# Forgetting attention on one core: the keys' low parts as two 64-row products side by side, pieces of a query tile in groups of two

## The chip, the cores and the metric

One core of a Trainium2 chip runs the whole kernel. The metric is device time in microseconds. The kernel before took 1963.35 us (median of 3 runs, 1961.30 to 1967.77); the profiled execution took 1961.69 us, with a span of 1960.3 us in the trace.

## What is computed

One layer of a hybrid decoder trunk on x of 2048 tokens by 1024 channels. The input projection feeds three mixers (trailing-window pooling, attention with a forget gate, a state-space layer), whose outputs are gated, lifted, merged and projected back, with a residual and a layer norm. The change touches the attention alone: 8 heads of 64 channels, causal, 128 queries at a time.

```python
scores = einsum('bqhd,bkhd->bhqk', qi, k) * scale        # scale = 1/sqrt(64)
bias = F[q] - F[k]                                       # F = cumsum(log sigmoid(f))
logits = where(key_pos <= q_pos, scores + bias, -inf)
p = softmax(logits)
out = einsum('bhqk,bkhd->bqhd', p, v)
```

## The kernel before

**Stages.** Three stages run one after the other: the projection with pooling and state space (until about 616 us), the attention (616 to 1552 us), and the merge with the output projection (to the end). The attention stage also carries 24 tiles of the gate projection in each of two phases: its matmuls fill the gaps that the attention leaves on TensorE, by a table of counts for each slot between the attention's steps (`fill_plan`, and `fill` in `head`). These fills write `g_ps`, 24 matmuls to a bank, each 128 rows by 512 columns.

**Split numbers.** Each fp32 operand is split in a high part that the fp32r format holds and a low part that is the rest. A product is high times high, plus high times low, plus low times high.

**Score products.** With 64 channels to a head, the 128 rows of the array hold a query tile twice. `q_st` has the high part of the scaled queries in rows 0 to 63 and their low part in rows 64 to 127. `k_hh` has the keys' high part in both halves, `k_ll` their low part in both halves. So one matmul `q_st` x `k_hh` (L1329) gives (high + low) x high, and a second one `q_st` x `k_ll` (L1330) adds (high + low) x low. Both have 128 rows. `q_tmp` is a third tile: its rows 64 to 127 hold the high part of the scaled queries, and serve only to work out the low part. `vT` lies in rows 0 to 63 of the same memory.

**Query tiles and pieces.** Query tile t (0 to 15) has (t + 1) * 128 keys, cut into pieces of 512 keys (`pieces`); the last piece can be 128, 256, 384 or 512 wide. That is one piece for t = 0 to 3, two for 4 to 7, three for 8 to 11, four for 12 to 15: 40 pieces to a head. A piece has a PSUM bank `s_ps` of three in turn. In `queries` (L1322 and on) TensorE waits until the bank is free, makes the two products, adds the causal mask to the tile's last 128 keys by a bf16 matmul with the identity (L1334), and signals `s_full`.

**The order around it.** In `head`, the loop over t has on TensorE, in this order: `queries` of tile t + 1, its first three pieces (L1412); the fills of slot (t, 0), eight or nine matmuls from t = 2 on; `queries` of tile t + 1, its fourth piece (L1415); for even t from 2 the products with the values of a pair of tiles (`values`, L1359, writing `o_ps`, closed by two transposes of `row_inv`, L1364); then `turn`, which transposes the probabilities of tile t by groups of four 128 by 128 fp32 transposes (L1345, writing `t_ps`, two banks in turn), with three fills between groups. The head begins with tile 0's queries, 16 transposes of `vT` (L1404), which has 64 rows only, and, in the second phase, the first fills.

**The other engines.** VectorE subtracts the key's forget sum from each piece and takes its maximum (`logits`, L1240, written to `s_sb`); it does all pieces of tile t + 1 before anything that it does for tile t's transposes. Behind them come the negated maximum (L1244), in some slots the split of a weight tile (L1230), then the low parts of the transposed probabilities (L1302), one for each piece, each after ScalarE's high part (L1208). ScalarE also takes the exponentials (L1199). The transposes of piece j in `turn` wait for the low part of the piece two before (the semaphore `t_lo`).

Of the kernel before, what the change touches and what calls it, by code (L numbers as in the profile page):

```python
# [25 lines left out]
P = 128  # L26
# [8 lines left out]
HD = 64  # L35
# [931 lines left out]
Q_TILES = S // P  # L967
# [8 lines left out]
def stage_attend(nc, io, scr, kept, ident, ident_b, mask, x_hi, x_lo, x_raw, gw_hi, gw_lo, gw_raw):  # L976
# [4 lines left out]
    with ExitStack() as ctx:  # L981
        def sb(name, shape, dt=F32):
            return ctx.enter_context(nc.sbuf_tensor(name, shape, dt))
# [6 lines left out]
        k_hh = sb("k_hh", [P, S], F32R)  # L990
        k_ll, q_st, q_tmp, vT, f_row = kept.k_ll, kept.q_st, kept.q_tmp, kept.vT, kept.f_row
# [10 lines left out]
        s_ps = [ctx.enter_context(nc.psum_tensor(f"s_ps{i}", [P, BANK], F32)) for i in range(3)]  # L1002
# [20 lines left out]
        def pieces(t):  # L1023

            n0 = sum(-(-(a + 1) // 4) for a in range(t))
            keys = (t + 1) * P
            return [(n0 + j, j * BANK, min(BANK, keys - j * BANK)) for j in range(-(-keys // BANK))]
# [5 lines left out]
        def pieces_to(t):  # L1033

            return pieces(t)[-1][0] + 1
# [284 lines left out]
        @block.tensor  # L1320
        def _(pe):
            def queries(at, t, part=slice(None)):  # L1322

                for n, k0, keys in pieces(t)[part]:
                    if n >= 3:
                        pe.wait_ge(s_free, at(S_PIECES, n - 2))
                    ps = s_ps[n % 3][:, 0:keys]
                    last_piece = k0 + keys == (t + 1) * P
                    pe.matmul(ps, q_st[:, t * P:(t + 1) * P], k_hh[:, k0:k0 + keys], start=True, stop=False)  # L1329
                    last = pe.matmul(ps, q_st[:, t * P:(t + 1) * P], k_ll[:, k0:k0 + keys], start=False,  # L1330
                                     stop=not last_piece)
                    if last_piece:

                        last = pe.matmul(ps[:, keys - P:keys], ident_b[:], mask[:], start=False, stop=True)  # L1334
                    last.then_inc(s_full, 1)

            def turn(at, t, fill):

                pe.wait_ge(p_ready, at(Q_TILES, t + 1))
                for j, (n, k0, keys) in enumerate(pieces(t)):  # L1340
                    if j:
                        fill((t, j))
                    pe.wait_ge(t_lo, at(PT_USES, n + 1))
                    for a in range(keys // P):
                        last = pe.transpose(t_ps[n % 2][:, a * P:(a + 1) * P],  # L1345
                                            s_sb[t % 2][:, k0 + a * P:k0 + (a + 1) * P], ident[:])
                    last.then_inc(t_full, 1)

            def values(at, p):

                pe.wait_ge(t_lo, at(PT_USES, pieces_to(2 * p + 1) + 2))
                if p:
                    pe.wait_ge(y_ready, at(8, p))
                last_key = 2 * p + 1
                for k in range(last_key + 1):

                    q = slice(P, 2 * P) if k == last_key else slice(0, 2 * P)
                    for j, pt in enumerate((pt_hi, pt_lo)):
                        pe.matmul(o_ps[:, 0, q], v_st[:, k, :], pt[:, k, q], start=(k == 0 and j == 0),  # L1359
                                  stop=(k == last_key and j == 1))  # L1360
                pe.wait_ge(inv_ready, at(8, p + 1))
                pe.sem_inc(passed[2])
                for a in range(2):
                    last = pe.transpose(o_ps[0:HD, 1, a * P:(a + 1) * P],  # L1364
                                        row_inv[:, 2 * p + a:2 * p + a + 1].broadcast_to([P, HD]), ident[:])
                last.then_inc(o_full, 1)

            def head(at, phase):

                    filled = [0]  # L1370

                    def fill(slot):
                        for _ in range(fill_counts[slot]):
                            piece, r = divmod(filled[0], 3 * KT)
                            j, c = divmod(piece, NCH)

                            k, (w, x) = ((r, (gw_hi, x_lo)) if r < KT else
                                         ((r - KT) // 2, ((gw_hi, x_hi), (gw_lo, x_hi))[(r - KT) % 2]))
                            filled[0] += 1
                            if r == 0:  # L1380
                                if c == 0:
                                    pe.wait_ge(gw_split, at(G_TILES, j + 1))
                                pe.wait_ge(g_ready, at(G_TILES * NCH, piece + 1))
                            if phase == 1 and j == 0 and r < KT:
                                pe.wait_ge(x2_split, c * KT + k + 1)
                            mm = pe.matmul(g_ps[c][:], w[j % 2][:, k, :], x[:, k, c * BANK:(c + 1) * BANK],  # L1386
                                           start=(r == 0), stop=(r == 3 * KT - 1))
                            if r == KT - 1:
                                mm.then_inc(x_lo_used, 1)
                            if r == 3 * KT - 1:  # L1390
                                mm.then_inc(g_done, 1)

                    if phase == 0:
                        fill("start")
                    pe.wait_ge(k_lo, at(1, 1))
                    pe.wait_ge(q_hi, at(1, 1))
                    pe.wait_ge(q_lo, at(1, 1))
                    queries(at, 0)
                    pe.wait_ge(v_loaded, at(16, 16))
                    pe.sem_inc(passed[2])  # L1400
                    for b in range(2):
                        for t in range(8):
                            k = 8 * b + t
                            last = pe.transpose(t_ps[b][:, t * HD:(t + 1) * HD], vT[:, k * P:(k + 1) * P],  # L1404
                                                ident[0:HD, 0:HD])
                        last.then_inc(t_full, 1)
                    if phase == 1:
                        fill("start")
                    for t in range(Q_TILES):

                        if t + 1 < Q_TILES:
                            queries(at, t + 1, slice(0, 3))  # L1412
                        fill((t, 0))
                        if t + 1 < Q_TILES:
                            queries(at, t + 1, slice(3, 4))  # L1415
                        if t % 2 == 0 and t >= 2:
                            values(at, t // 2 - 1)
                        turn(at, t, fill)
                    fill("end")
                    values(at, 7)  # L1420
                    fill("tail")

            pe.sem_inc(g_ready, NCH)  # L1423
            for phase in range(2):
                with pe.Fori(0, PHASE_HEADS - phase) as i:
                    head(lambda k, c: i * k + (c + phase * PHASE_HEADS * k), phase)
            head(lambda k, c: (HEADS - 1) * k + c, 1)


# [455 lines left out]
```

## Time and profile before

| | |
|---|---|
| median of 3 runs | 1963.35 us |
| profiled execution, its time | 1961.69 us |
| its span in the trace | 1960.3 us |
| TensorE, busy share of the span | 98% |
| VectorE | 57% |
| ScalarE | 36% |
| GpSimd | 22% |
| granted TensorE clock, mean | 0.995 |

The trace names each matmul (PE) and each weight load (PEld) with its start. A matmul's end is modelled and laps over the next one's start, so what a matmul costs in a dense stretch is the distance from its start to the next start, not its printed duration. The printed shape `128*128 128x512` is the stationary tile (rows*columns), then the moving tile; `64*128` is a stationary tile of 64 rows.

### The profile page before, as it was taken

Reading aid. Unit: us, or ns where it says so; the run is one execution under the profiler, and the core shown is the slowest. Engines: PE = TensorE matmul, PEld = TensorE weight load, DVE = VectorE, ACT = ScalarE, POOL = GpSimd, SP = SyncE. Lnnn points to the kernel's source line nnn. Section 1 sums busy time; section 2 is a strip of 40 time slices with the busy share of each in tenths; the row PEclk is TensorE's granted clock in tenths of the full one; section 3 lists DMA queues with packets and bytes.
Section 4 is the critical chain, followed back from the end, with each engine's and each line's share of the span. In section 5 each row is a group of like instructions: output and inputs, shape, how many; then the busy total and the mean of one; then the engine's idle time right before and its main releaser. Section 6 shows DMA issues by size and latency. Waiting matters only on the chain. (4 is left out here: it accounts for less than half of the span.)

```text
span 1960.3 us, 30528 instructions
## 1 busy us (share of the span) xinstructions
PE 1913.3 (98%) x10560; PEld 1623.1 (83%) x10560; DVE 1124.5 (57%) x2133; ACT 706.6 (36%) x1081; POOL 435.0 (22%) x548
## 2 busy tenths in 40 slices
PE   7999999999999999999999999999999989999998
PEld 6878887888887888888888788888888878999997
DVE  4564235654245655646465665565645568777776
ACT  3121013021034555555555655455555541111110
POOL 2927930498000000000000000000000002222322
PEclk9999999999999999999999999999999989999999
DMA  7124225322432151231423515133142276555542
GB/s 190 67 86 118 86 86 196 63 107 107 139 109 93 49 139 54 80 110 47 138 68 87 175 48 139 62 87 109 49 128 66 91 251 209 170 173 171 174 118 86
DMA packets 103479, 221.68 MB, mean 113 GB/s; under 512 B 10936, under 2 KB 56680, under 8 KB 99816
## 3 DMA queue, kind: packets, MB, share of 16 engines
q1 hardware_dynamic: 89648, 161.41, 26.2%
q0 software_dynamic: 12608, 55.19, 10.1%
q10 hardware_dynamic: 1152, 4.19, 0.5%
q8 instruction: 37, 0.61, 0.1%
q14 instruction: 34, 0.28, 0.0%
HBM read 155.09 MB, written 65.08 MB: 112 GB/s over the span
## 5 line engine op out<-in xcount | busy, mean ns | idle before, releaser
L1386 PE MATMUL g_ps<-x_hi,w_lo 128*128 128x512 f32 x768 | 309.4, 403 | 0.0
L1386 PE MATMUL g_ps<-x_hi,w_hi 128*128 128x512 f32 x768 | 308.4, 402 | 0.0
L1302 DVE TENSOR_TENSOR pt_lo<-t_ps,pt_hi 128x512 fp32r<-128x512 f32 (+2 forms) x320 | 190.4, 606 | 138.2 <-ACT pt_hi L1208 137.8
L643 PE MATMUL tile_ps<-x_hi,w_hi 128*128 128x512 f32 x752 | 234.1, 393 | 11.2 <-DVE x_lo L362 11.2
L643 PE MATMUL tile_ps<-x_hi,w_lo 128*128 128x512 f32 x752 | 232.1, 390 | 0.0
L643 PE MATMUL tile_ps<-x_lo,w_hi 128*128 128x512 f32 x752 | 232.0, 390 | 0.0
L1386 PE MATMUL g_ps<-x_lo,w_hi 128*128 128x512 f32 x768 | 225.9, 410 | 3.9 <-PEq L1423 2.6
L1208 ACT ACTIVATE pt_hi<-t_ps 128x512 fp32r<-128x512 f32 (+2 forms) x320 | 170.4, 533 | 142.4 <-PE t_ps L1345 137.9
L1240 DVE CUSTOM_DVE_ANT_0 s_sb<-s_ps,f_row 128x512 f32<-128x512 f32 (+2 forms) x320 | 181.6, 604 | 35.1 <-PE s_ps L1334 34.4
L1116 POOL DMA_DIRECT2D mixT<-y_out x63 | 33.8, 536 | 748.1 <-DVE y_out L1254 748.1
L1345 PE MATMUL t_ps<-ident,s_sb 128*128 128x128 f32 x1088 | 172.1, 273 | 9.6 <-DVE pt_lo L1302 5.2
L643 PEld LDWEIGHTS tile_ps<-x_hi,w_hi 128*128 128x128 f32 x752 | 141.1, 188 | 41.5 <-issue 12.6
L1345 PEld LDWEIGHTS t_ps<-ident,s_sb 128*128 128x128 f32 x1088 | 133.2, 140 | 47.1 <-DVE pt_lo L1302 10.8
L280 ACT ACTIVATE w_hi<-w_lo_raw 128x1024 fp32r<-128x1024 f32 x49 | 52.0, 1061 | 319.9 <-DMA w_lo_raw<-in_w_tiles 319.9
L1386 PEld LDWEIGHTS g_ps<-x_hi,w_lo 128*128 128x128 f32 x768 | 145.4, 189 | 24.9
L643 PEld LDWEIGHTS tile_ps<-x_lo,w_hi 128*128 128x128 f32 x752 | 141.4, 188 | 29.6
L643 PEld LDWEIGHTS tile_ps<-x_hi,w_lo 128*128 128x128 f32 x752 | 141.5, 188 | 29.5
L1386 PEld LDWEIGHTS g_ps<-x_hi,w_hi 128*128 128x128 f32 x768 | 145.4, 189 | 24.6
L1386 PEld LDWEIGHTS g_ps<-x_lo,w_hi 128*128 128x128 f32 x768 | 136.3, 190 | 28.5 <-PEq L1423 3.1
L1199 ACT ACTIVATE s_sb<-s_sb,neg_max 128x128 f32<-128x128 f32 (+15 forms) x128 | 153.3, 1197 | 6.7 <-DVE neg_max L1244 6.6
L1733 PE MATMUL u_ps<-y_hi,wu_hi 128*128 128x256 f32 x512 | 146.1, 285 | 9.0 <-DVE gate L1662 6.4
L1733 PE MATMUL u_ps<-y_lo,wu_hi 128*128 128x256 f32 x512 | 146.0, 285 | 0.0
(276 smaller groups left out, 3537.4 us busy)
## 6 DMA issues: line engine op xcount, KB each, us to landing
w_lo_raw<-in_w_tiles SPq DMA_DIRECT2D x96, 512.0 KB, 3.6
gateT<-g_out SPq DMA_DIRECT2D x96, 256.0 KB, 3.0
gate<-gateT SPq DMA_DIRECT2D x64, 384.0 KB, 4.5
x_lo_raw<-in_xT SPq DMA_DIRECT2D x24, 512.0 KB, 8.4
qkvT<-zout SPq DMA_DIRECT2D x24, 512.0 KB, 3.2
silT<-zout SPq DMA_DIRECT2D x16, 512.0 KB, 2.7
k_ll<-qkvT POOLq DMA_DIRECT2D x16, 512.0 KB, 6.7
q_st<-qkvT POOLq DMA_DIRECT2D x16, 512.0 KB, 8.7
```

The source lines that it names most:

```text
L280: act.activation(w_hi[par][:], w_raw[par][:], ACT.Copy).then_inc(w_split_hi, 1)
L643: last = pe.matmul(tile_ps[par][:, c * BANK:(c + 1) * BANK], w[par][:, k, :], x[:, k, c * BANK:(c + 1) * BANK], start=(k == 0 and j == 0), ...
L1116: pool.dma_start(scr["mixT"][bass.ds(row, HD), p * 2 * P:(p + 1) * 2 * P], y_out[p % 2][:]).then_inc(y_stored, 16)
L1199: act.activation(row, row, ACT.Exp, bias=neg_max[t % 2][:], accum_out=row_sum[:, t:t + 1]).then_inc(p_ready, 1)
L1208: act.activation(pt_hi[:, k0 // P:(k0 + keys) // P, (t % 2) * P:(t % 2 + 1) * P], t_ps[n % 2][:, 0:keys].rearrange("p (k q) -> p k q", q=P ...
L1240: dve.tensor_tensor_reduce(s_sb[t % 2][:, k0:k0 + keys], s_ps[n % 3][:, 0:keys], f_row[:, k0:k0 + keys], 1.0, -3e38, ALU.subtract, ALU.max ...
L1302: dve.tensor_tensor(pt_lo[part], t_ps[n % 2][:, 0:keys].rearrange("p (k q) -> p k q", q=P), pt_hi[part].bitcast(F32), ALU.subtract).then_i ...
L1345: last = pe.transpose(t_ps[n % 2][:, a * P:(a + 1) * P], s_sb[t % 2][:, k0 + a * P:k0 + (a + 1) * P], ident[:])
L1386: mm = pe.matmul(g_ps[c][:], w[j % 2][:, k, :], x[:, k, c * BANK:(c + 1) * BANK], start=(r == 0), stop=(r == 3 * KT - 1))
L1733: mm = pe.matmul(u_ps[d % 2][:, n, :], w, y[:, k, :], start=(k == k0 and j == 0), stop=(k == k1 - 1 and j == 2))
```

## The change

`queries` takes the pieces of a call as a group. First it makes the products with `k_hh` of all pieces of the group, 128 rows each, as before. Then, where the group has one piece, the product with `k_ll` follows as before. Where it has two, the keys' low part is multiplied with the queries' high part alone: for the first piece in rows 0 to 63 (stationary from `q_st`), for the second in rows 64 to 127 (stationary from `q_tmp`). The product low times low is left out there. The mask follows at the end. The calls in `head` take pieces 0 and 1 ahead of the fills of slot (t, 0), and pieces 2 and 3 behind them, where it was 0 to 2 and 3.

```diff
             def queries(at, t, part=slice(None)):
 
-                for n, k0, keys in pieces(t)[part]:
+                group, q = pieces(t)[part], slice(t * P, (t + 1) * P)
+                for n, k0, keys in group:
                     if n >= 3:
                         pe.wait_ge(s_free, at(S_PIECES, n - 2))
+                    pe.matmul(s_ps[n % 3][:, 0:keys], q_st[:, q], k_hh[:, k0:k0 + keys], start=True, stop=False)
+                for i, (n, k0, keys) in enumerate(group):
                     ps = s_ps[n % 3][:, 0:keys]
                     last_piece = k0 + keys == (t + 1) * P
-                    pe.matmul(ps, q_st[:, t * P:(t + 1) * P], k_hh[:, k0:k0 + keys], start=True, stop=False)
-                    last = pe.matmul(ps, q_st[:, t * P:(t + 1) * P], k_ll[:, k0:k0 + keys], start=False,
-                                     stop=not last_piece)
-                    if last_piece:
-
-                        last = pe.matmul(ps[:, keys - P:keys], ident_b[:], mask[:], start=False, stop=True)
-                    last.then_inc(s_full, 1)
+                    if len(group) == 1:
+                        last = pe.matmul(ps, q_st[:, q], k_ll[:, k0:k0 + keys], start=False, stop=not last_piece)
+                    else:
+                        q_hi, rows = ((q_st, slice(0, HD)), (q_tmp, slice(HD, P)))[i]
+                        last = pe.matmul(ps, q_hi[rows, q], k_ll[rows, k0:k0 + keys], start=False, stop=not last_piece)
+                    if not last_piece:
+                        last.then_inc(s_full, 1)
+                n, k0, keys = group[-1]
+                if k0 + keys == (t + 1) * P:
+
+                    pe.matmul(s_ps[n % 3][:, keys - P:keys], ident_b[:], mask[:], start=False, stop=True).then_inc(s_full, 1)
...
                         if t + 1 < Q_TILES:
-                            queries(at, t + 1, slice(0, 3))
+                            queries(at, t + 1, slice(0, 2))
                         fill((t, 0))
-                        if t + 1 < Q_TILES:
-                            queries(at, t + 1, slice(3, 4))
+                        if t + 1 >= 8 and t + 1 < Q_TILES:
+                            queries(at, t + 1, slice(2, 4))
```

On TensorE, tile 5 of a head, whose two pieces are 512 and 256 keys wide (its one group). `s_ps` is the piece's bank. Before:

```order
L1326 REGISTER_ALU
L1329 MATMUL s_ps<-k_hh,q_st 128x512 [waits s_free]
L1330 MATMUL s_ps<-k_ll,q_st 128x512
L1326 REGISTER_ALU
L1329 MATMUL s_ps<-k_hh,q_st 128x256 [waits s_free]
L1330 MATMUL s_ps<-k_ll,q_st 128x256
L1334 MATMUL s_ps<-mask,ident_b 128x128
```

and in the changed program:

```order
L1327 REGISTER_ALU
L1328 MATMUL s_ps<-k_hh,q_st 128x512 [waits s_free]
L1327 REGISTER_ALU
L1328 MATMUL s_ps<-k_hh,q_st 128x256 [waits s_free]
L1336 MATMUL s_ps<-k_ll,q_st 128x512
L1336 MATMUL s_ps<-k_ll,q_tmp 128x256
L1342 MATMUL s_ps<-mask,ident_b 128x128
```

The two products with the low part now stand side by side, behind both products with the high part. The printed shapes are those of the output; the two L1336 matmuls read 64 rows each.

On TensorE, tile 14 of a head, from the last fill of slot (13, 0) to tile 13's first transposes. Before:

```order
L1386 MATMUL g_ps<-x_hi,w_lo 128x512
L1326 REGISTER_ALU
L1329 MATMUL s_ps<-k_hh,q_st 128x384 [waits s_free]
L1330 MATMUL s_ps<-k_ll,q_st 128x384
L1334 MATMUL s_ps<-mask,ident_b 128x128
L1339 REGISTER_ALU
L1343 REGISTER_ALU [waits p_ready]
L1345 MATMUL t_ps<-ident,s_sb 128x128 [waits t_lo]
```

and in the changed program:

```order
L1393 MATMUL g_ps<-x_hi,w_lo 128x512
L1327 REGISTER_ALU
L1328 MATMUL s_ps<-k_hh,q_st 128x512 [waits s_free]
L1327 REGISTER_ALU
L1328 MATMUL s_ps<-k_hh,q_st 128x384 [waits s_free]
L1336 MATMUL s_ps<-k_ll,q_st 128x512
L1336 MATMUL s_ps<-k_ll,q_tmp 128x384
L1342 MATMUL s_ps<-mask,ident_b 128x128
L1346 REGISTER_ALU
L1350 REGISTER_ALU [waits p_ready]
L1352 MATMUL t_ps<-ident,s_sb 128x128 [waits t_lo]
```

The third piece of the tile has moved from ahead of the fills to behind them, directly before the transposes. VectorE's instructions stand in the same order in both programs.

## Rows read from the trace of the kernel before

**Rows 1.** The page, busy time of TensorE, its share, and instructions.

```profile
PE 1913.3 (98%) x10560; PEld 1623.1 (83%) x10560; DVE 1124.5 (57%) x2133; ACT 706.6 (36%) x1081; POOL 435.0 (22%) x548
```

**Rows 2.** Busy time in one stretch (us, engines, then PEclk, DMA): the attention stage.

```profile
616.00:1552.00 936.00, 925.57 (x5379) 779.43 (x5377) 539.92 (x1357) 507.98 (x825) 55.28 (x104) 1.00 0.31 90
```

**Rows 3.** Waits of TensorE, 620 to 1552 us: who, for whom, us, times, longest.

```profile
PE t_ps L1345 <- DVE pt_lo L1302: 5.2, 8, 1.2
PE t_ps L1345 <- ACT s_sb L1199: 3.9, 7, 0.6
```

**Rows 4.** Timeline of PE (start us, duration): scores of tile 14 after a transpose.

```profile
1177.77 0.33 PE L1345 MATMUL t_ps<-ident,s_sb 128*128 128x128 f32 x1
1177.86 0.50 PE L1329 MATMUL s_ps<-k_hh,q_st 128*128 128x512 f32 x1
1178.19 0.39 PE L1330 MATMUL s_ps<-k_ll,q_st 128*128 128x512 f32 x1
1178.42 0.40 PE L1329 MATMUL s_ps<-k_hh,q_st 128*128 128x512 f32 x1
```

**Rows 5.** Timeline of PE: tile 0's scores, then the first 64-row matmul.

```profile
736.60 0.22 PE L1329 MATMUL s_ps<-k_hh,q_st 128*128 128x128 f32 x1
736.66 0.28 PE L1330 MATMUL s_ps<-k_ll,q_st 128*128 128x128 f32 x1
736.78 0.23 PE L1334 MATMUL s_ps<-mask,ident_b 128*128 128x128 bf16 x1
736.94 0.27 PE L1404 MATMUL t_ps<-ident,vT 64*128 64x64 f32 x1
```

**Rows 6.** Timeline of PE: the last three 64-row matmuls, then tile 1's scores.

```profile
737.80 0.34 PE L1404 MATMUL t_ps<-ident,vT 64*128 64x64 f32 x3
738.07 0.39 PE L1329 MATMUL s_ps<-k_hh,q_st 128*128 128x256 f32 x1
738.30 0.28 PE L1330 MATMUL s_ps<-k_ll,q_st 128*128 128x256 f32 x1
738.42 0.23 PE L1334 MATMUL s_ps<-mask,ident_b 128*128 128x128 bf16 x1
```

**Rows 7.** Timeline of weight loads: the first into 64 rows, the first behind them.

```profile
736.94 0.20 PEld L1404 LDWEIGHTS t_ps<-ident,vT 64*128 64x128 f32 x2
...
738.07 0.19 PEld L1329 LDWEIGHTS s_ps<-k_hh,q_st 128*128 128x128 f32 x1
```

**Rows 8.** Timeline of PE: tile 14's last piece, mask, tile 13's first transposes.

```profile
1181.38 0.34 PE L1330 MATMUL s_ps<-k_ll,q_st 128*128 128x384 f32 x1
1181.56 0.23 PE L1334 MATMUL s_ps<-mask,ident_b 128*128 128x128 bf16 x1
1181.63 0.61 PE L1345 MATMUL t_ps<-ident,s_sb 128*128 128x128 f32 x4
```

**Rows 9.** Timeline of weight loads at the places of rows 4 and 8.

```profile
1177.85 0.19 PEld L1329 LDWEIGHTS s_ps<-k_hh,q_st 128*128 128x128 f32 x1
1177.96 0.19 PEld L1330 LDWEIGHTS s_ps<-k_ll,q_st 128*128 128x128 f32 x1
...
1181.57 0.42 PEld L1345 LDWEIGHTS t_ps<-ident,s_sb 128*128 128x128 f32 x4
```

**Rows 10.** Timeline of VectorE around the transposes of tile 13 (in brackets its idle time).

```profile
1179.43 0.69 DVE L1240 CUSTOM_DVE_ANT_0 s_sb<-s_ps,f_row 128x512 f32<-128x512 f32 x1
...
1180.04 0.69 DVE L1240 CUSTOM_DVE_ANT_0 s_sb<-s_ps,f_row 128x512 f32<-128x512 f32 x1
...
1181.98 0.56 DVE L1240 CUSTOM_DVE_ANT_0 s_sb<-s_ps,f_row 128x384 f32<-128x384 f32 x1 [1.25 <-PE s_ps L1334]
...
1182.68 1.23 DVE L1230 TENSOR_TENSOR w_lo<-w_lo_raw,w_hi 128x1024 fp32r<-128x1024 f32 x1
...
1183.90 1.27 DVE L1302 TENSOR_TENSOR pt_lo<-t_ps,pt_hi 128x512 fp32r<-128x512 f32 x2
```

**Rows 11.** Timeline of PE: the third group of transposes of tile 13.

```profile
1184.62 0.66 PE L1345 MATMUL t_ps<-ident,s_sb 128*128 128x128 f32 x4 [0.56 <-DVE pt_lo L1302]
```

## The prediction

> **What bounds the kernel now.** I read the busy shares first. TensorE is busy for 98% of the span [rows 1] and for 925.6 of the 936 us of the attention stage, at the full granted clock of 1.00, which is the 2.4 GHz level [rows 2]; VectorE has 540 us of work there, ScalarE 508. Then the waits: TensorE loses 5.2 us to VectorE's `pt_lo` and 3.9 us to ScalarE's exponentials in the whole stage [rows 3]. So the attention stage is a queue of TensorE work without holes, and what the change takes from or adds to that queue shows in the time one for one. The third view is the timeline of starts, because printed durations lap over each other. A 512-column matmul costs 0.23 us from start to start (1178.19 to 1178.42) [rows 4], a 384-column one 0.18 [rows 8], a 256-column one 0.12 (738.30 to 738.42) [rows 6], a 128-column one 0.06 (736.60 to 736.66) [rows 5]. The fourth view is the weight loads, because the change makes the array go between 128-row and 64-row work, and the trace before has one place in each head that does this: the `vT` transposes.
>
> **How many pairs.** From `pieces`: tiles 4 to 7 give one pair each, tiles 8 to 11 one (the third piece stands alone), tiles 12 to 15 two. That is 16 to a head, 128 in 8 heads. In 80 of them both pieces are 512 wide; in 16 each the second is 384, 256 or 128 wide. 64 pairs (tiles 4 to 7, and the second pair of 12 to 15) are followed by the mask, 64 by another fp32r matmul. Everything else in the stage keeps its matmuls.
>
> **What a pair saves.** If the two halves run side by side, they take as long as the wider one plus the lag of the second. No row shows two 64-row matmuls in different halves. I bound the lag at 0 below and, above, at one exposed fp32r weight load: 0.11 us, by the two loads that follow one another at 1177.85 and 1177.96 [rows 9] and by the 0.23 us that the first 256-column matmul takes at 738.07 where the next takes 0.12 [rows 6]. I take 0.11, since the second load has to follow the first on the same engine.
> - 512 and 512: 0.46 before, 0.23 + 0.11 = 0.34 after, 0.12 saved.
> - 512 and 384: 0.23 + 0.18 = 0.41 before, 0.11 + 0.18 = 0.29 after, 0.12 saved.
> - 512 and 256: 0.35 before, 0.23 after, 0.12 saved.
> - 512 and 128: the 128-wide product takes 0.12 ahead of the mask (736.66 to 736.78) [rows 5], so 0.35 before, 0.23 after, 0.12 saved.
>
> 128 x 0.12 = **15.4 us saved**. With no lag it would be 80 x 0.23 + 16 x (0.18 + 0.12 + 0.12) = 25.1 us.
>
> **What a pair costs: two switches.** Into 64 rows: the mask matmul starts at 736.78, and the first weight load into 64 rows starts only at 736.94, together with its matmul, 0.16 us later [rows 5, 7]. The same mask matmul ahead of full 128-row transposes: 1181.56, then the transpose at 1181.63, 0.07 us later, its weights loading from 1181.57 [rows 8, 9]. So 0.09 us is waited before the load. On top the load itself is exposed: the first `vT` matmul is 0.27 long, and the later ones 0.22 (0.34 for three that start 0.06 apart) [rows 5, 6]: 0.05. Entry: 0.14 us; with a full fp32r load exposed, 0.09 + 0.11 = 0.20. Out of 64 rows: the last `vT` matmul starts at 738.14 - 0.22 = 737.92; the next load and matmul start at 738.07, 0.15 later instead of 0.06 [rows 6, 7], so 0.09 again; and the matmul behind has its load exposed, 0.11 (above). Exit: 0.20 us; into the mask, whose bf16 load is short, I take 0.15 (0.09, and half of the 0.11, rounded up).
>
> Part of the exposed load on the way out may belong to the change from fp32 transposes to fp32r: behind full-height transposes the first score product also takes 0.33 instead of 0.23 (1177.86 to 1178.19) [rows 4]. So the lower bound of a switch is the wait alone, 0.09 each way, 0.18 to a pair; the upper is 0.20 each way, 0.40. I take 0.14 + 0.20 for 64 pairs and 0.14 + 0.15 for 64: 64 x 0.34 + 64 x 0.29 = **40.3 us added**. I stay near the upper bound because in both rows the load did not start before the wait was over, and a load that has not started early is exposed. The bounds are 128 x 0.18 = 23.0 and 128 x 0.40 = 51.2 us.
>
> What I read in these rows is also a rule. The Trainium skill (TensorEngine Tiling (Array Packing), Key Properties) says that changing the tiling mode, not merely the tile, makes TensorE drain. The trace agrees, with 0.09 us of waiting each way. The skill's other page (TensorE: Matmul & The Clock Gate, Measured speedup vs the span model) has row-packed matmuls starting some 4 ns apart and 64-row work overlapping freely; by that figure alone the sum would be an estimated 25 us saved, less about half a microsecond. No run here shows that lag yet.
>
> **What moves.** The products with `k_hh` of a group come first, so the first piece's `s_full` comes some 0.4 us later. VectorE starts later on it, but it idles there for longer than that (1.25 us before 1181.98) [rows 10]. In tiles 8 to 11 the third piece, and in 12 to 15 the third of four, goes behind the eight or nine fills of slot (t, 0). No TensorE work is added by this, but VectorE, which must finish tile t + 1 before tile t's `pt_lo`, gets its last pieces in a bunch. For even t the products with the values, over 2 us, stand behind and cover it. For t = 7, 9 and 11 ScalarE's high part is not ready much before VectorE is free, and the third transpose group is due about 2.4 us after the first (from 1181.63 to 1184.62 less 0.56) [rows 8, 11]: covered, narrowly. For t = 13 it is not: a weight split of 1.23 us stands in VectorE's way, and TensorE already waits 0.56 us [rows 10, 11], once in each head (8 times) [rows 3]. There a 512-wide piece (0.61 us from start to start, 1179.43 to 1180.04 [rows 10]) is added behind the mask: 8 x 0.61 = **4.9 us added**; 0 if VectorE finds slack, twice that if tile 11 stalls too.
> The waits of GpSimd for the head's last `s_full` and `s_free` move with the pieces by less than 1 us; its loads for the next head have the head's end as cover. No DMA, no ScalarE and no VectorE instruction is added. The 3.9 us of waiting for exponentials stand at tile 15, which has no queries behind it, and stay.
>
> **Sum.** -15.4 + 40.3 + 4.9 = +29.8 us on the profiled 1961.69: **1991.5 us**. The median of the runs shown is 1.7 us higher, well under 0.3% (5.9 us), about what a measurement of this kernel can tell from no change. Its own bounds: -25.1 + 23.0 + 0 = -2, and -15.4 + 51.2 + 9.8 = +46; with the terms leaning together only in part, 1972 to 2003.
>
> **Rivals.**
> 1. *The switches are nearly free (faster).* The gaps at the `vT` transposes would come from what surrounds them: a change of data type with unprefetched loads (the full-height transposes show such a 0.10 on the way out [rows 4]) and the wait for `v_loaded`. Two fp32r matmuls of 64 rows behind fp32r ones of 128 would then have none. For it: entry and exit at `vT` are never free of a change of type. Against it: the mask to the full-height transposes is a change of type too and has no 0.16 gap [rows 8]. Time: -15.4 + 4.9 = -10.5, 1951 us; without lag and stall -25, 1937. It decides where a switch costs under 0.06 us (0.12 saved, shared by two).
> 2. *Wash.* A switch costs about 0.09 and the second half starts with little lag: between -6 and +6 us, about 1963.
> 3. *The halves do not overlap (much slower).* If TensorE runs the two 64-row matmuls one after the other, nothing is saved and both switches are paid: 40.3 + 4.9 = +45, 2007 us, up to 2018. Nothing in the trace before speaks for or against; the second matmul's `s_full` would then come a full 0.23 us behind the first's in the 512-wide pairs. That is the case in which the change does not do what it says.
>
> **How the numbers follow.** Switches that cost more than the pair saves: 0.57 (own range 1972 to 2003). Free switches: 0.25. Wash: 0.12. No overlap: 0.06. Slower by over 0.3% takes the first and the last, less a little for the first's low bound, 0.62; the wash gives "same" 0.13 with that; faster 0.25. The range has to reach into the free switches: from 1945 to 2006, which leaves out the lower tail of that rival and most of the last.
>
> **What would show it.** In the changed profile, at a 512 and 512 pair followed by fills: the weight load of the first 64-row matmul starts some 0.3 us behind the start of the second `k_hh` matmul (not within it); the second 64-row matmul starts 0.11 us behind the first; the fill behind has its load start about 0.3 us after the last 64-row matmul. From the start of the second `k_hh` matmul to the second fill I expect about 1.1 us, where the free case gives 0.8. The count of matmuls stays at 10560 and their printed durations change little, so the loss must show in distances and in TensorE's idle or unattributed time. VectorE's `pt_lo` as a releaser of TensorE should go from 5.2 to about 10 us. I am wrong if the load of the 64-row matmul starts inside the matmul ahead of it, or if the two halves start over 0.2 us apart.

## The result, and the profile after

The changed kernel takes 1985.26 us (median of 4 runs, 1984.74 to 1985.63) against 1963.01 us before (four runs now): ratio 1.0107, 95% interval 1.0094 to 1.0120, so 22 us slower. The profiled execution took 1984.74 us with a span of 1983.4 us, 23.1 us over the span before.

The page of the changed kernel, busy times, which answer to [rows 1]:

```profile
PE 1930.5 (97%) x10560; PEld 1592.4 (80%) x10560; DVE 1131.2 (57%) x2133; ACT 706.7 (36%) x1081; POOL 435.5 (22%) x548
```

The same number of matmuls. TensorE's printed busy time rises by only 17 us, and its share falls by a point. Its waits, 620 to 1572 us (who, for whom, us, times, longest), which answer to [rows 3]:

```profile
PE t_ps L1352 <- DVE pt_lo L1302: 8.2, 8, 1.1
PE t_ps L1352 <- ACT s_sb L1199: 3.9, 7, 0.6
```

The named waits grew by 3.0 us. The rest of the 23 us has no releaser, so it must lie in distances between starts. This is the timeline of PE around the two pairs of tile 15 (start us, duration); it answers to [rows 4, 8] with the 64-row matmuls in it. The first two pieces stand ahead of the fills, the last two ahead of the mask and the products with the values:

```profile
1201.28 0.40 PE L1328 MATMUL s_ps<-k_hh,q_st 128*128 128x512 f32 x1
1201.61 0.49 PE L1336 MATMUL s_ps<-k_ll,q_st 64*128 64x512 f32 x1
1201.61 0.50 PE L1336 MATMUL s_ps<-k_ll,q_tmp 64*128 64x512 f32 x1
1202.04 0.50 PE L1393 MATMUL g_ps<-x_hi,w_lo 128*128 128x512 f32 x1
1202.38 0.40 PE L1393 MATMUL g_ps<-x_lo,w_hi 128*128 128x512 f32 x1
...
1204.24 0.39 PE L1328 MATMUL s_ps<-k_hh,q_st 128*128 128x512 f32 x1
1204.56 0.49 PE L1336 MATMUL s_ps<-k_ll,q_st 64*128 64x512 f32 x1
1204.57 0.49 PE L1336 MATMUL s_ps<-k_ll,q_tmp 64*128 64x512 f32 x1
1204.99 0.23 PE L1342 MATMUL s_ps<-mask,ident_b 128*128 128x128 bf16 x1
```

And the weight loads of the same stretch, where "issue" stands for idle time with no releaser:

```profile
1201.61 0.18 PEld L1336 LDWEIGHTS s_ps<-k_ll,q_st 64*128 64x128 f32 x1 [0.36 <-issue]
1201.61 0.18 PEld L1336 LDWEIGHTS s_ps<-k_ll,q_tmp 64*128 64x128 f32 x1
1202.04 0.19 PEld L1393 LDWEIGHTS g_ps<-x_hi,w_lo 128*128 128x128 f32 x1 [0.25 <-issue]
1202.15 1.59 PEld L1393 LDWEIGHTS g_ps<-x_lo,w_hi 128*128 128x128 f32 x7
```

Read it from left to right. The two halves start within 0.01 us of each other, here as in all 128 pairs: they do run side by side. But the weights of the first 64-row matmul are loaded 0.32 to 0.33 us behind the start of the `k_hh` matmul ahead of it, where a matmul that needs no switch starts 0.23 us behind and has had its weights loaded earlier. On the way out the next load starts 0.43 us behind the pair, and the fill it belongs to lasts 0.34 us instead of 0.23 (1202.04 to 1202.38), since its load was exposed. From the second `k_hh` matmul to the second fill it is 1.10 us; before, the same work was one `k_hh`, two `k_ll` and one fill, 4 x 0.23 = 0.92. So this pair loses 0.18 us. Ahead of the mask the pair needs 0.75 us (1204.24 to 1204.99) instead of 0.69, and loses 0.06.

The best ruler for the whole is the distance between two heads. The 16 `vT` transposes stand at a fixed place in each head. Before:

```profile
1337.36 1.20 PE L1404 MATMUL t_ps<-ident,vT 64*128 64x64 f32 x16
1457.92 1.20 PE L1404 MATMUL t_ps<-ident,vT 64*128 64x64 f32 x16
```

and in the changed kernel:

```profile
1355.46 1.20 PE L1411 MATMUL t_ps<-ident,vT 64*128 64x64 f32 x16
1478.87 1.20 PE L1411 MATMUL t_ps<-ident,vT 64*128 64x64 f32 x16
```

A head takes 120.56 us before and 123.41 us after: 2.85 us more. The seven distances between heads grow by 20.2 us together, the last head with all that follows it by 2.1, and what stands ahead of the first head by 0.8. So nearly all of the loss is made in the heads.

The stall at tile 13, in the changed kernel, timeline of PE:

```profile
1198.23 0.40 PE L1393 MATMUL g_ps<-x_hi,w_lo 128*128 128x512 f32 x1
1199.64 0.66 PE L1352 MATMUL t_ps<-ident,s_sb 128*128 128x128 f32 x4 [1.01 <-DVE pt_lo L1302]
```

From the last fill to the transposes it is 1.41 us. Before, that fill stands at

```profile
1183.67 0.40 PE L1386 MATMUL g_ps<-x_hi,w_lo 128*128 128x512 f32 x1
```

and the transposes at 1184.62 [rows 11], 0.95 us. The stall cost 0.46 us more in this head, and as much in each of the first seven. In the last head it was longer before, 1.63 us from start to start, and is 1.46 now. So the stalls grew by 3.0 us in all, as the named waits did.

### The profile page after: what moved, and what is told of

Its sections match the earlier page's. It is cut to its first block and busy times, and to the rows that moved or that the text cites. A ratio compares the mean times of both kernels' runs of the same rounds, so it can differ in the third digit from the quotient of the medians.

```text
span 1983.4 us, 30528 instructions
## 1 busy us (share of the span) xinstructions
PE 1930.5 (97%) x10560; PEld 1592.4 (80%) x10560; DVE 1131.2 (57%) x2133; ACT 706.7 (36%) x1081; POOL 435.5 (22%) x548
```

## The experiments

Each row gives the median, its ratio to the kernel before on the same chip, and the length of a head in the one profile of each kernel (the distance of the last two rows of `vT` transposes, as above). In one profile that length repeats within 0.3 us, but for the two distances around the change of phase and, in the last kernel, the first one.

| kernel | median us | ratio, 95% interval | head, us |
|---|---|---|---|
| before | 1963 to 1964 | 1 | 120.56 |
| changed | 1985.26 | 1.0107, 1.0094 to 1.0120 | 123.41 |
| order only | 1964.96 | 1.0007, 0.9996 to 1.0017 | 120.80 |
| both products in one half | 2006.17 | 1.0218, 1.0201 to 1.0235 | 126.16 |
| pair issued twice | 2014.63 | 1.0259, 1.0241 to 1.0276 | 127.14 |
| 64 rows alone, no pair | 1980.46 | 1.0083, 1.0067 to 1.0100 | 122.64 |
| pairs at the mask only | 1973.68 | 1.0046, 1.0032 to 1.0059 | 121.88 |
| low part first | 1985.57 | 1.0109, 1.0093 to 1.0124 | 123.30 |
| split moved, on before | 1957.03 | 0.9966, 0.9952 to 0.9979 | 119.83 |
| split moved, on changed | 1978.82 | 1.0072, 1.0059 to 1.0086 | 122.32 |
| split and fills moved, on before | 1956.41 | 0.9967, 0.9957 to 0.9977 | 119.71 |

**Order only.** The rival to "the switches cost" was that the new order does. So the changed kernel's order, without a 64-row matmul:

```diff
-                    if len(group) == 1:
+                    if True:
                         last = pe.matmul(ps, q_st[:, q], k_ll[:, k0:k0 + keys], start=False, stop=not last_piece)
```

> The changed kernel's order (groups of two, both products with k_hh first, pieces 2 and 3 behind the fills), but every product with k_ll on all 128 rows, so no 64-row matmul in the scores. Theory (the two switches of the array cost more than the pair saves): only VectorE's stall at tile 13 is left over from the change, 3 us more than before, so 1966 us, and 19 us under the changed kernel. Rival (the loss is the order: VectorE gets its pieces in a bunch and late, and TensorE waits on it in places that the waits do not name): 1980 to 1985 us.

Measured: 1964.96 us, not told apart from the kernel before; the head is 0.24 us longer, 1.9 us in 8. Its waits, 620 to 1620 us:

```profile
PE t_ps L1352 <- DVE pt_lo L1302: 8.1, 8, 1.6
```

The longer stall at tile 13 is there too, and it is all that the order costs: from the last fill to the transposes it is 1.32 us in that kernel's timeline against 0.95 before, 0.37 more. Of this 0.06 and 0.08 us to a head come back ahead of the first transposes of tiles 7 and 9, where a mask that stood ahead of fills now stands directly ahead of the transposes. The 20 us belong to the 64-row matmuls.

**Both products in one half.** Same switches, no overlap:

```diff
-                        q_hi, rows = ((q_st, slice(0, HD)), (q_tmp, slice(HD, P)))[i]
+                        q_hi, rows = (q_st, slice(0, HD))
```

> The changed kernel, but the second 64-row product of a pair also works in rows 0 to 63, so that the two cannot overlap and the count of switches stays. Theory (the halves do overlap fully, lag 0.01 us): each pair gets longer by its second product, 80 x 0.23 + 16 x (0.18 + 0.12 + 0.06) = 24 us, so 2009 us. Rival (they share some port, or the pair is bound by weight loads, and overlap only in part): 1986 to 2000 us.

Measured: 2006.17 us, 21 us over the changed kernel; the head is 2.75 us longer, 22 us in all. That is what the overlap is worth here, close to the 24 expected. 1.6 of the missing 2 us are VectorE's stall, which shrank to 6.6 us. So the pair does what it is meant to do.

**Pair issued twice.** This counts the low-part product of the paired pieces twice, to price a pair without a switch of its own:

```diff
+                if len(group) == 2:
+                    for i, (n, k0, keys) in enumerate(group):
+                        q_hi, rows = ((q_st, slice(0, HD)), (q_tmp, slice(HD, P)))[i]
+                        pe.matmul(s_ps[n % 3][:, 0:keys], q_hi[rows, q], k_ll[rows, k0:k0 + keys], start=False,
+                                  stop=False)
                 for i, (n, k0, keys) in enumerate(group):
```

> The changed kernel with each pair of 64-row products issued twice in a row (the low-part product is counted twice, so the scores are off by one more low-part product). Theory (the cost sits in the two switches, not in the 64-row matmuls): the second pair of halves costs only its streaming, 128 x 0.23 = 29 us, so 2015 us. Rival (each 64-row matmul pays a wait of its own, 0.43 from pair to next load): 128 x 0.43 = 55 us, 2040 us.

Measured: 2014.63 us, on the number; the head is 3.73 us longer, 0.233 us to a pair. The timeline of PE at one of them:

```profile
1218.58 0.49 PE L1332 MATMUL s_ps<-k_ll,q_st 64*128 64x512 f32 x1
1218.59 0.50 PE L1332 MATMUL s_ps<-k_ll,q_tmp 64*128 64x512 f32 x1
1218.92 0.39 PE L1341 MATMUL s_ps<-k_ll,q_st 64*128 64x512 f32 x1
1218.92 0.39 PE L1341 MATMUL s_ps<-k_ll,q_tmp 64*128 64x512 f32 x1
1219.24 0.50 PE L1398 MATMUL g_ps<-x_hi,w_lo 128*128 128x512 f32 x1
```

The first pair takes 0.34 us, the 0.23 of a 512-column matmul and an exposed load. The second takes 0.32 us up to the fill, the same 0.23 and then 0.09 of waiting for the way out. Between the two pairs nothing is lost; the price is paid where 128-row and 64-row work meet.

**64 rows alone.** The disputed price by itself, in the kernel before, where nothing is paired (low times low is left out in these 64 products):

```diff
-                    last = pe.matmul(ps, q_st[:, t * P:(t + 1) * P], k_ll[:, k0:k0 + keys], start=False,
+                    alone = slice(0, HD) if last_piece and (t < 4 or 8 <= t < 12) else slice(None)
+                    last = pe.matmul(ps, q_st[alone, t * P:(t + 1) * P], k_ll[alone, k0:k0 + keys], start=False,
```

> The kernel before, with its own order, where the low-part product of the one piece of tiles 0 to 3 and of the third piece of tiles 8 to 11 is made on 64 rows alone (64 products in all; low times low is left out in them). Nothing is paired and nothing is saved, so this prices two switches by themselves. Theory: for a 512-wide piece 0.32 + 0.43 = 0.75 us from its k_hh product to the mask instead of 0.46, for a 128-wide one 0.42 instead of 0.18; some 0.28 x 64 = 18 us, 1981 us. Rival (switches are nearly free, the loss of the change lies elsewhere): 1963 us.

Measured: 1980.46 us; the head is 2.08 us longer for 8 such products, 0.26 us each. A 512-wide one, timeline of PE:

```profile
1247.11 0.47 PE L1329 MATMUL s_ps<-k_hh,q_st 128*128 128x512 f32 x1
1247.51 0.50 PE L1331 MATMUL s_ps<-k_ll,q_st 64*128 64x512 f32 x1
1247.94 0.23 PE L1335 MATMUL s_ps<-mask,ident_b 128*128 128x128 bf16 x1
```

The same 0.43 us from the 64-row matmul to the mask as in a pair. One 64-row matmul takes as long as a pair, and a switch in and out costs some 0.26 us even ahead of the cheap mask. The rival of free switches is out.

**Pairs at the mask only.** Do all pairs lose alike?

```diff
-                    if len(group) == 1:
+                    if len(group) == 1 or group[-1][1] + group[-1][2] < (t + 1) * P:
```

> The changed kernel with 64-row pairs only where the mask follows (tiles 4 to 7, and pieces 2 and 3 of tiles 12 to 15); the other 64 pairs, all 512 and 512, make their low-part products on 128 rows. Theory (the way out costs less into the bf16 mask than into an fp32r matmul: 0.06, 0.11, 0.17, 0.17 us a pair for a second piece of 512, 384, 256, 128, against 0.17 for the others): 16 x 0.51 = 8.2 us over the order-only kernel, 1973 us. Rival (every pair costs the same, 20 / 128 us): 1975 us; if the pairs with a narrow second piece carry all of the loss: 1983 us.

Measured: the head is 1.08 us longer than in the order-only kernel, 8.6 us in all, 0.135 us a pair; 0.08 us of the 1.08 is the stall at tile 13, which is 1.41 us here as in the changed kernel. The other 64 pairs make up the difference to the changed kernel, 1.53 us a head, 0.19 us a pair. The first agrees with the 8.2 us worked out from the rows, the second with the 0.18 read off above. In time (1973.68 against 1965) the theory and its rival are only 2 us apart, and it is the head's length that tells them apart.

**Low part first.** If a weight load behind the fp32 transposes is exposed anyway, a pair set there should pay for its entry only in part:

```diff
+                two = len(group) == 2 and group[-1][1] + group[-1][2] < (t + 1) * P
+                if two:
+                    for i, (n, k0, keys) in enumerate(group):
...
+                        pe.matmul(s_ps[n % 3][:, 0:keys], q_hi[rows, q], k_ll[rows, k0:k0 + keys], start=True, stop=False)
```

> The changed kernel, but in the 64 pairs that stand directly behind a turn's fp32 transposes and have no mask (pieces 0 and 1 of tiles 8 to 15), the two 64-row products come first and the two products with k_hh behind them. Theory (a weight load exposed behind the transposes is paid anyway, 0.10 us, so the entry there costs only its wait): 64 x 0.10 = 6.4 us fewer, 1979 us. Rival (each switch pays its own full price wherever it stands): 1985 us.

A miss: 1985.57 us, no gain. The timeline of PE at tile 15:

```profile
1202.64 0.38 PE L1362 MATMUL t_ps<-ident,s_sb 128*128 128x128 f32 x2
1202.95 0.49 PE L1331 MATMUL s_ps<-k_ll,q_st 64*128 64x512 f32 x1
1202.96 0.50 PE L1331 MATMUL s_ps<-k_ll,q_tmp 64*128 64x512 f32 x1
1203.39 0.74 PE L1335 MATMUL s_ps<-k_hh,q_st 128*128 128x512 f32 x2
1203.96 0.39 PE L1403 MATMUL g_ps<-x_hi,w_lo 128*128 128x512 f32 x1
```

The last transpose starts at 1202.75 (1202.64 + 0.38 less the 0.27 that one lasts), the pair's load 0.20 us later, where transposes follow each other 0.11 us apart: the same wait of 0.09. From the last transpose to the first fill it is 1.21 us. In the changed kernel the last transpose starts at 1200.94, the fill at 1202.04 with 0.11 us of exposed load: 1.21 us too. So there was no 0.10 us to share. I had read it from the 0.33 us behind the recorded start of a `k_hh` matmul [rows 4], but that start is recorded early, with its load, while the transpose ahead is still at work. The distance from the transpose shows it. Before, at tile 15, timeline of PE:

```profile
1185.82 0.38 PE L1345 MATMUL t_ps<-ident,s_sb 128*128 128x128 f32 x2
1185.95 0.47 PE L1329 MATMUL s_ps<-k_hh,q_st 128*128 128x512 f32 x1
1186.26 0.39 PE L1330 MATMUL s_ps<-k_ll,q_st 128*128 128x512 f32 x1
```

The two transposes are 0.38 - 0.27 = 0.11 us apart, so the second starts at 1185.93, and the second score product 0.33 us behind it: no more than the 0.11 of a transpose and the 0.23 of a score product. The type change costs nothing that these rows can show. In rows 4 the same distance is 0.42 us, since the single transpose there has its own load exposed (0.33 long instead of 0.27).

**Split moved.** VectorE's weight split at tile 13 goes behind the four `pt_lo`:

```diff
                     for j in splits((t, 0), last):
-                        split_w(at, j)
+                        if t != 13:
+                            split_w(at, j)
...
+                    if t == 13:
+                        for j in splits((t, 0), last):
+                            split_w(at, j)
```

On the kernel before:

> The kernel before, with the one change that at tile 13 VectorE splits the weight tile behind its four pt_lo instead of ahead of them. Theory (the stall of TensorE at tile 13 is made by that split, and the queue has no other hole there): 8 x 0.56 = 4.5 us fewer, 1959 us. Rival (VectorE is late anyway, or the fills behind miss their weights): 1963 us or more.

and on the changed kernel:

> The changed kernel with the same move of the weight split at tile 13. Theory (the bunched pieces and the split together make the 8.2 us of waits on pt_lo): these waits go nearly to nothing, 1977 us. Rival (the third piece behind the fills is late by itself): 3 to 5 us of them stay, 1981 us.

Measured: 1957.03 and 1978.82 us, on both sides faster than without; the head is 0.73 us shorter on before and 1.09 us on the changed kernel, 5.8 and 8.7 us in all. TensorE's waits on `pt_lo` in the two, 620 to 1620 us:

```profile
PE t_ps L1349 <- DVE pt_lo L1303: 0.6, 1, 0.6
```

```profile
PE t_ps L1356 <- DVE pt_lo L1303: 0.3, 1, 0.3
```

The split was the main cause in both. The gain is larger than the printed wait of 0.56 us: from start to start the stall before was 0.95 - 0.23 = 0.72 us, and that is what came back. On the changed kernel 1.09 of 1.18 us came back: from start to start it is 0.33 us there now, so 0.10 us of the stall is left. With the stalls nearly away the change costs 122.32 - 119.83 = 2.49 us a head, 20 us: the switches less what the pairs save.

**Split and fills moved**, towards a version that beats both kernels further. In the table of fills:

```diff
+    counts[12, 0] -= 3
+    counts[15, 0] += 3
```

> The kernel before with the split moved at tile 13, and three fills moved from slot (12, 0) to slot (15, 0), where TensorE waits 4.4 us in all (8 times) for the exponentials. Theory (what VectorE and ScalarE make TensorE wait is all that can be had from the order, and a wait printed as 0.56 costs 0.72 from start to start, since ends are modelled): the second stall goes too, 8 x 0.72 = 5.8 us under the 1957 us of the kernel with the split moved alone, 1951 us. Rival (the three fills are missed at tile 12, where the wait comes back): 1955 us or more.

The rival's time came true: 1956.41 us, the same as with the split alone, though the wait came back at tile 13's transposes and not at tile 12. The wait for the exponentials fell from 4.4 to 0.6 us and the one for `pt_lo` came back with 4.6 us. ScalarE's and VectorE's timelines at tile 13:

```profile
1300.23 1.06 ACT L1152 ACTIVATE w_hi<-w_lo_raw 128x1024 fp32r<-128x1024 f32 x1 [2.05 <-DMA w_lo_raw<-in_w_tiles]
1301.19 1.06 ACT L1210 ACTIVATE pt_hi<-t_ps 128x512 fp32r<-128x512 f32 x2
```

```profile
1301.81 1.29 DVE L1305 TENSOR_TENSOR pt_lo<-t_ps,pt_hi 128x512 fp32r<-128x512 f32 x2 [0.99 <-ACT pt_hi L1210]
```

Three fills fewer ahead of tile 13 finish the gate tile later, so its weight buffer is reloaded later, ScalarE waits for that load in line ahead of its `pt_hi` (2.05 us here, 0.92 at the same place with the split alone), and the chain ends at the same transposes. The kernel before with the split moved stays as good as any version here: 0.34% under before (0.21 to 0.48).

## Why the prediction was right, and where its sizes were off

The direction, the mechanism and the place were right; the time was 6 us below the forecast and inside the likeliest case's own range. That it came so near is in part luck: the saving and the switches were both put too low, by 10 us and by 4 to 6, and these errors cancel in part.

| term | predicted, us | measured, us |
|---|---|---|
| saved by the pairs | 15.4 | 25, the sum with no lag |
| two switches, 128 times | 40.3 | 44 to 46 |
| stall at tile 13 | 4.9 | 3.0 |
| sum | +29.8 | +22.3 (medians) |

**What a pair saves** was the term most off. The step that failed is "the second load has to follow the first on the same engine", which made a lag of 0.11 us. The lag is 0.01 or less: the two loads of 64 rows start together. So the saving is the upper bound of 25.1 us, and the products in one half bear it out (22 us lost, with 1.6 us less of the stall). The Trainium skill (TensorE: Matmul & The Clock Gate, Measured speedup vs the span model) counts some 4 ns for each further packed matmul, and the rows here agree with it, as far as 0.01 us can tell.

**The switches.** A head got 2.85 us longer; with the stall's 0.46 us off and the saved 25.1 / 8 = 3.14 us on, 5.53 us are left for 16 pairs, 0.346 us each, 44 us in all; measured from the order-only kernel it is (123.41 - 120.80 + 3.14) / 16 = 0.36. Read from the rows it is 0.41 us for a pair ahead of a fill (1.10 - 3 x 0.23) and 0.29 ahead of the mask (0.75 - 2 x 0.23), 64 of each, 45 us. I had 0.34 and 0.29. The entry was undersized: 0.09 us of waiting (0.32 less the usual 0.23), as predicted, but the full exposed load of 0.11, which makes 0.20, not 0.14. The exit ahead of an fp32r matmul was right, 0.20 (0.43 less 0.11 and 0.23, and the load of 0.11). The exit into the mask was oversized, 0.09 for 0.15, and so the 0.29 came out right by luck. The Trainium skill (TensorEngine Tiling (Array Packing), Key Properties) says that a change of tiling mode drains the array. Every run with a switch agrees: the next load starts 0.09 us later than the usual distance, both ways, while between two pairs it does not wait at all. That the wait is a drain is the skill's word for it; the runs show the wait alone.

**My lower bound for a switch**, the wait alone, rested on the step that part of the exposed load "may belong to the change from fp32 transposes to fp32r". The low-first run shows that it does not, and the distance from the last transpose would have shown it in the trace before. That bound was far too kind to the change, and so was the chance of 0.12 for a wash.

**What moves.** TensorE's stall on VectorE grew by 0.46 us and not by 0.61 because the third piece's `s_full` now comes with the 64-row matmul, ahead of the mask, so VectorE starts 0.16 us earlier relative to the mask than before (0.26 us behind the mask's start, where it was 0.42). In the last head it shrank by 0.17 us, and the term is 3.0 us, not 4.9. That no other tile stalls, tile 11 above all, was right: 8 waits on `pt_lo`, one in each head. The order costs nothing else that shows.

**The rivals.** Free switches are refuted by the 64-row products alone (+17 us with nothing paired), and no overlap by the products in one half. The wash had the small lag right and the switches too cheap. Of the signs that I named two came true: the load 0.32 us behind the `k_hh` matmul, 1.10 us from there to the second fill. Three did not: the second half stood 0.01 us and not 0.11 behind the first, the fill's load 0.43 us and not 0.3 behind the last 64-row matmul, and the waits for `pt_lo` came to 8.2 us and not to 10.

## What to carry to other kernels

On an array that is busy without holes, price a half-height pair as one matmul saved against two switches, each of which costs a wait and most times a weight load that nothing hides: here 0.23 us against some 0.35. The second of two pairs in a row costs its streaming alone (the pair issued twice), so by these figures two useful pairs between the same two switches would save 0.46 us against 0.35; that is worked out, and no run here has it. And before a stall is blamed on a long engine, look what stands in its queue by choice: moving one weight split was worth 6 us, where the change cost 22.

## What the runs showed that I had not expected

Across the halves, matmuls do not keep the order of the program. With the pair issued twice and a 256-wide second piece, the second `q_tmp` matmul starts ahead of the second `q_st` matmul that is issued before it, 0.22 us behind the first matmul in its own half. In that kernel's timeline of PE:

```profile
1201.37 0.49 PE L1332 MATMUL s_ps<-k_ll,q_st 64*128 64x512 f32 x1
1201.38 0.38 PE L1332 MATMUL s_ps<-k_ll,q_tmp 64*128 64x256 f32 x1
1201.60 0.28 PE L1341 MATMUL s_ps<-k_ll,q_tmp 64*128 64x256 f32 x1
1201.71 0.39 PE L1341 MATMUL s_ps<-k_ll,q_st 64*128 64x512 f32 x1
```

The program issues `q_st` before `q_tmp` both times; the second round starts at 1201.60 and 1201.71 in the other order. It is so in all 48 pairs of that kernel whose second piece is narrower, and in none of the 80 with equal pieces. Until it is tried, a semaphore on the later-issued matmul of such a pair should not be taken to cover the earlier-issued one in the other half; here the unmasked piece has a signal of its own, and the mask, which starts 0.33 us behind the last of them, has the other. Whether completion can be reordered too was not tried.
